# Unread products in front of the modulation groups' transposes, in a two-block transformer kernel

## What is computed

```python
def squared_relu_mlp(h, w_up, w_down):
    a = jax.nn.relu(h @ w_up)
    return (a * a) @ w_down
...
def ada_modulation(c, ada_w, ada_b):
    m = jax.nn.silu(c) @ ada_w + ada_b
    return jnp.split(m, N_MOD, axis=-1)
...
def swiglu(h, w_gate, w_up, w_down):
    return (jax.nn.silu(h @ w_gate) * (h @ w_up)) @ w_down
...
def even_layer(x, c, ada_w, ada_b, ...):
    sh_m, sc_m, g_m, sh_f, sc_f, g_f = ada_modulation(c, ada_w, ada_b)
    h = modulate(rms_norm(x, mix_norm), sh_m, sc_m)
...
    x = x + g_m[:, None, :] * y
    hf = modulate(rms_norm(x, ffn_norm), sh_f, sc_f)
    return x + g_f[:, None, :] * swiglu(hf, ffn_w_gate, ffn_w_up, ffn_w_down)
```

## Time and profile before

| | us |
|---|---|
| median of 3 runs | 1194.04 |
| lowest, highest | 1193.58, 1200.17 |
| the profiled execution | 1198.31 |
| its span in the trace | 1196.7 |
| TensorE busy in the span | 1181.8 |
| VectorE busy | 865.3 |
| ScalarE busy | 636.4 |

### The profile page before, as it was taken

One profiled execution on the slowest core, in us unless ns is written; L12 is line 12 of the kernel. 1 busy time (PEld: TensorE's weight loads), 2 busy tenths in 40 slices (PEclk: granted clock), 3 DMA queues, 4 the chain that ended last, 5 costly groups with the idle time before them and its releaser, 6 DMA issues.

```text
span 1196.7 us, 23369 instructions
## 1 busy us (share of the span) xinstructions
PE 1181.8 (99%) x9635; PEld 1146.2 (96%) x9635; DVE 865.3 (72%) x1148; ACT 636.4 (53%) x854; POOL 95.6 (8%) x147
## 2 busy tenths in 40 slices
PE   8999999999999999999999999999999999999998
PEld 8999999999998999999999999999988779999998
DVE  5776888778786788777889988886476557845443
ACT  7557566624337567634368463443455665543332
POOL 0000011110115011111100001110000000000000
PEclk9999999999999999999999999999999999999999
DMA  9452588887772488778754557876645505565352
GB/s 335 160 171 77 176 289 273 287 289 259 272 259 77 150 279 307 256 289 302 268 199 142 179 173 255 284 264 226 218 160 184 168 1 174 179 210 164 125 192 82
DMA packets 150298, 250.00 MB, mean 209 GB/s; under 512 B 5537, under 2 KB 80906, under 8 KB 150218
## 3 DMA queue, kind: packets, MB, share of 16 engines
q1 hardware_dynamic: 136098, 198.21, 49.4%
q0 software_dynamic: 13952, 50.60, 11.7%
q10 hardware_dynamic: 168, 0.04, 0.0%
HBM read 247.79 MB, written 1.05 MB: 208 GB/s over the span
## 4 chain that ended last, share of the span: by engine, by line
PE 92%; DVE 5%; ACT 1%; issue 1%; ACTq 0%; POOL 0%; DVEq 0%
PE ps L2155 27%; PE ps L2157 27%; PE ps L2156 27%; DVE w_lo L1257 2%; PE ps L2423 2%; PE ps L2293 1%; PE ps L2734 1%; PE ps L2405 1%; PE ps L2209 1%; PE ps L2708 1%; PE ps L2392 1%; PE ps L2748 1%; PE ps L2236 0%; PE ps L2391 0%; ACT h_both L808 0%
## 5 line engine op out<-in xcount | busy, mean ns | idle before, releaser
L1257 DVE TENSOR_TENSOR w_lo<-raw,w_hi 128x2048 fp32r<-128x2048 f32 (+4 forms) x196 | 412.7, 2144 | 102.0 <-ACT w_hi L741 101.7
L741 ACT ACTIVATE w_hi<-raw 128x2048 fp32r<-128x2048 f32 (+4 forms) x196 | 342.0, 1790 | 168.2 <-PE ps L2157 168.2
L2155 PE MATMUL ps<-h_both,w_hi 128*128 128x256 f32 (+1 forms) x1296 | 363.5, 280 | 3.1 <-issue 1.1
L2157 PE MATMUL ps<-h_both,w_lo 128*128 128x256 f32 (+1 forms) x1296 | 361.1, 279 | 0.0
L2156 PE MATMUL ps<-h_both,w_hi 128*128 128x256 f32 (+1 forms) x1296 | 361.1, 279 | 0.0
L2155 PEld LDWEIGHTS ps<-h_both,w_hi 128*128 128x128 f32 (+1 forms) x1296 | 242.7, 187 | 4.6 <-issue 2.8
L2156 PEld LDWEIGHTS ps<-h_both,w_hi 128*128 128x128 f32 (+1 forms) x1296 | 245.0, 189 | 0.1
L2157 PEld LDWEIGHTS ps<-h_both,w_lo 128*128 128x128 f32 (+1 forms) x1296 | 243.1, 188 | 0.0
L2155 PE MATMUL ps<-a_both,w_hi 128*128 128x256 f32 x864 | 241.7, 280 | 0.0
L2156 PE MATMUL ps<-a_both,w_hi 128*128 128x256 f32 x864 | 240.8, 279 | 0.0
L2157 PE MATMUL ps<-a_both,w_lo 128*128 128x256 f32 x864 | 240.8, 279 | 0.0
(11 more groups left out here) (422 smaller groups left out, 1823.5 us busy)
## 6 DMA issues: line engine op xcount, KB each, us to landing
ada_raw<-in_l_ada_w POOLq DMA_DIRECT2D x96, 512.0 KB, 6.5
raw<-in_mlp_w_up SPq DMA_DIRECT2D x32, 1024.0 KB, 6.6
raw<-in_mlp_w_down SPq DMA_DIRECT2D x32, 1024.0 KB, 7.0
raw<-in_l_ffn_w_gate SPq DMA_DIRECT2D x22, 1024.0 KB, 5.5
raw<-in_l_ffn_w_up SPq DMA_DIRECT2D x22, 1024.0 KB, 8.0
raw<-in_l_ffn_w_down SPq DMA_DIRECT2D x16, 768.0 KB, 5.7
raw<-in_l_w_qkv SPq DMA_DIRECT2D x12, 1024.0 KB, 6.7
raw<-in_l_w_in SPq DMA_DIRECT2D x10, 1024.0 KB, 6.5
```

The lines of the kernel that those rows point to most:

```text
L741: nc.scalar.activation(w_hi[:, s.slot, cut], raw[:, s.slot, cut], ACT.Copy).then_inc(split_hi, 1)
L1257: nc.vector.tensor_tensor(w_lo[:, s.slot, cut], raw[:, s.slot, cut], w_hi[:, s.slot, cut].bitcast(F32), ALU.subtract).then_inc(split_lo, 1)
L2155: nc.tensor.matmul(to, sh, mh, start=first, stop=False, skip_group_check=True)
L2157: return nc.tensor.matmul(to, sl, mh, start=False, stop=last, skip_group_check=True)
```

## The change

In front of the four transposes of a group, one more product is issued, into the same bank. The transposes overwrite it, and nothing reads it. Its stationary operand is the first 128 columns of the running slot's `w_hi`, its moving operand the first 252, 244, 254, 240 or 250 columns of the running stage's activations, by a table with one number for each stage. It is given at the 18 calls of `two_bank_slot` and of the downward loops; the six other calls stay as they were.

```diff
+UNREAD = {"up0": 252, "down0": 244, "up1": 254, "down1": 240, "gate_up0": 250}
...
-            def ada_reduce(group):
+            def ada_reduce(group, unread=None):
 
                 pe.wait_ge(ada_step, group * 8 + 8)
+                if unread is not None:
+
+                    w, x, n = unread
+                    nc.tensor.matmul(ps[:, ADA_BANK, 0:n], w, x[:, 0:n], start=True, stop=True, skip_group_check=True)
                 for q in range(4):
                     ins = nc.tensor.transpose(ps[:, ADA_BANK, q * P:(q + 1) * P],
                                               scratch[:, 2 + q // 2, (q % 2) * P:(q % 2 + 1) * P], ident[:, :])
...
                     if b and reduce is not None:
-                        ada_reduce(reduce)
+                        ada_reduce(reduce, (ring(w_hi, s.slot, s.kc, s.cols)[:, 0, 0:P], hi[:, 0, :], UNREAD[phase]))
...
                             if b == 1 and j % 2 == 0:
-                                ada_reduce(ADA_GROUP[f"down{l}"] + 2 * i + j // 2 - 1)
+                                ada_reduce(ADA_GROUP[f"down{l}"] + 2 * i + j // 2 - 1,
+                                           (ring(w_hi, s.slot, s.kc, s.cols)[:, 0, 0:P], a_hi[:, KD * j, :], UNREAD[f"down{l}"]))
```

## The result

The changed kernel takes 1199.61 us (median of 19 runs), the kernel before 1195.20 us (19 runs as well): a ratio of 1.0038, 95% interval 1.0023 to 1.0054. The medians are 4.4 us apart; by the ratio, which is estimated over all the runs and not from the medians, it is 4.5 us slower, between 2.7 and 6.5. The forecast was 3.1 us quicker, with a range that ended at 1199.0 us. It had the wrong sign.

The account below looks back on a forecast made before the run. TensorE, busy for 99% of the span, was taken as the bound. Products +2.0, faster stretches -7.0, groups 8 and 23 +0.2 and +1.7 sum to -3.1 us: from the median 1194.04 to 1191.0 us, range 1186.0 to 1199.0.

Parts of the forecast that it names:

- The bound: Whole kernel: TensorE, busy for 99% of the span, sets the end, which moves almost one for one with its stream.
- Two paces, kept until something interrupts: TensorE's product stream runs at about 113.4 or 117.8 ns a step until a group of transposes interrupts it.
- The exact moment at which the group begins: At each group of transposes: this moment, not the instructions, decides which pace follows; no size of its own.
- The product's own price: The 18 added products on TensorE: 0.113 us each, 2.0 us in all; 3.9 us at the upper bound.
- Both bounds: Limits for one added product: 112 ns from 128-column products below, 215 ns from plain fp32 products of 256 columns above.
- rival 4: A short added product costs 215 ns: 1.9 us on top of any case, 1197.9 us with pace unturned; chance 0.1.
- I take it that a group moved by a product falls as they did: Covered groups, shifted one product, leave fast like groups 11 and 19; all 18 followed by the fast pace gains 7.0 us.
- rival 3: Every covered group is left slow, slow arrivals spoiled too: +9.1 us, 1203.1 us; chance 0.12.
- some flip each way: Covered stretches, part of the unturned-pace rival (0.23 together): some change pace in either direction, mixed cases between 1191 and 1200 us.
- Late next: Uncovered groups 8 and 23, now entered fast, should leave slow as nine of eleven did: 0.2 and 1.7 us lost.
- The reference: Starting time: median 1194.04 us of the runs shown, profiled run 1198.31; the last loop's 5.6 us could differ between runs.
- an unturned pace: Covered stretches go on in turn, the added product changing no pace: +2.0 us, 1196.0 us; chance 0.23 including mixed cases.

Follow-up runs that it names:

- as_products: Kernel before with four 256-column products in place of the four transposes of each of the 18 covered groups, nothing in front: 1189.37 us, ratio 0.9955.
- all256: Changed kernel with 256 columns in all 18 added products: 1197.92 us, ratio 1.0026.
- before_third: Third trace of the kernel before, no edit: span 1199.0 us.
- after_again: Second trace of the changed kernel, no edit: span 1207.0 us.

## Why the prediction was wrong

**The bound: right.** TensorE's stream is the end; the trace of the change shows no idle time in front of any of the 18 products, and windows of equal work differ by the pace alone.

**Two paces, kept until something interrupts: right, and now shown.** as_products takes the transposes away, and the pace stands for 150 us. The earlier trace rows had already given both sizes. "The exact moment at which the group begins" deciding the outcome was less well founded: the last steps before a group measure 117 or 118 ns in the kernel before whether quick stays quick or turns slow.

**The product's own price: right, its bounds misread.** Forecast 0.113 us each and 2.0 in all; measured 0.107 to 0.118, 2.0 us. Both bounds came from the earlier trace rows, which are plain fp32 products, and the kernel's text issues half as many as there are records: 6 for the 12 records of L2242, one for the two of L2555, two for the four of L2557. So such a product takes about 225 ns with 128 columns and 430 with 256; 112 and 215 ns are a record's. The bound from below said nothing of the float32r type, and the one from above was half of the product's. The middle value of the forecast did not rest on either; rival 4, and with it the upper end of the range, rests on the 215.

**"I take it that a group moved by a product falls as they did": this is the step that failed.** I read the two quick-to-quick groups, 11 and 19, as arrivals at another moment, and a product as the shift that would bring this moment about for all. all256 makes exactly this shift, and the pattern stays that of the kernel before. In the change itself only 9 of 24 quick arrivals stayed quick, where the forecast needed all. I counted the nearest cases, two of them, and gave half of the chance to what they suggested; before_third has two more, at groups 1 and 11, behind the same code that turned slow in other traces. So being the first group of a loop did not give the quick outcome either.

**What stood in its place** was in my own rows. Ten passages out of ten had taken a slow stream to a quick one: that was the good half of the turn, and the change put something in front of just these. I priced its loss only as rival 3, in which all 18 are slow (0.12), and let "some flip each way" lie between 1191 and 1200 without asking which flips could be had. The quick-to-slow passages were bad in nine cases of eleven already and could gain; the slow-to-quick ones, ten out of ten, could only lose. What happened is the loss of the second without much of the first: 21 of 30 slow passages stay slow, and of the quick ones 9 of 24 stay quick, against 4 of 31.

**Late next: the case did not arise.** The 0.2 and 1.7 us were for groups 8 and 23 entered quick. Group 8 was entered slow in all three traces of the change and left quick. Group 23 was entered slow twice, left quick once and slow once (after_again, 1.7 us: four bare transposes that did not turn a slow stream), and entered quick once and left quick. Over the traces of all kernels in which these two groups kept their four bare transposes, they left slow in 9 of the 18 cases in which they were entered quick, not in nine of eleven.

**The reference: better judged than used.** I wrote that the last loop could be the difference of 5.6 us from run to run; it is, between the first two traces, and it fits the two clusters of single times. It should have made the range wider on the upper side by itself: 1196.0 for an unturned pace and half of 5.6 us is 1198.8, so the range's end had no room for a single slow stretch more. The median of three runs was low as well: 1194.04 where 19 runs gave 1195.20, 1.2 us, more than the 0.6 us by which the result lies above the range. That moves the number; the sign was wrong by the passages.

What stays open is why two paces exist and what decides at a group which of them follows. The runs show which passages turn and which keep; they do not show the mechanism. The step into the first transposition (110 to 124 ns) does not separate the outcomes, as shown above, and none of the runs set it alone. Each variant but the two kernels was traced once, and the single times were taken on several chips, so the counts are those of these traces and not rates.

## What to carry to other kernels

Where one engine bounds a kernel without idle time, read the distance between starts, stretch by stretch: equal work in two times, with no wait, clock or other engine behind it, can mean that the stream has two paces, and a trace that shows one of them is one draw. Before changing what stands at an interruption, make the table of passages, what came in and what went out, and ask which of its cells can still get better and which can only get worse. And where a stage untouched by the change can move the whole by more than the change is worth, compare stages, and take several traces, before trusting a total.

## What the runs showed of the hardware

- A stream of float32r products of 128 x 128 by 256 columns at the full clock of 2.4 GHz runs at 113.3 or at 117.8 ns a product, and holds either for at least 1260 products; the 4% between them were worth 5.6 us in one loop. The Trainium skill (TensorE: Matmul & The Clock Gate, Back-to-back issue gap) gives columns over 2.4 plus 2.5 ns as the gap of isolated products, an estimated 109 ns for 256 columns, and says that in a stream of weight loads and products both set the spacing, 81 ns at 128 columns and 131 ns at 512. No stretch of 256-column products of this case runs at the 109 ns, and float32r products of 512 columns come 229 ns apart (median of 317 steps in the first trace of before); the measurement decides.
- Four fp32 transposes of 128 x 128 interrupt it; in the 18 places of the kernel before, out of slow they gave quick 23 times of 23, out of quick they gave slow 27 times of 31. Bare at groups 8 and 23, over the traces of all kernels, they left quick 14 times of 15 out of slow, but slow only 9 times of 18 out of quick. Four products of the stream's own type and size in their place changed no pace at 18 places of one trace.
- A float32r product of 240 to 254 columns in front of them costs 107 to 118 ns, nearly what one of 256 does (113 or 121), but changes the passage: 244 columns kept slow slow 25 times of 26. Behind the transposes 244, 250 and 254 columns kept quick quick in all 18 places of one trace each.
- A plain fp32 product of 128 columns stands in the trace as two records 112 ns apart, 224 ns together, where the fp32 transposition of the same operands takes 109 ns; one of 256 columns stands as two records 215 ns apart, 430 ns together.
